# One layer of a hybrid decoder on one core: a per-layer product moved forward, and two late loads put behind the final gathers

## What is computed

```python
u = rmsnorm(h, norm_ffn)
# top group of 4, then top 2 of the 4 experts in it, weights `combine`
for e in range(N_EXPERTS):                      # 16 experts, width 256
    gu = u @ w_gate_up[e]
    hid = silu(gu[..., :D_EXPERT]) * gu[..., D_EXPERT:]
    moe = moe + combine[..., e:e+1] * (hid @ w_down[e])
h = h + moe
u = rmsnorm(h, norm_ple)                        # the per-layer input embedding
gate = sigmoid(u @ w_ple_gate)                  # 1024 x 1024
h = h + gate * (p @ w_ple_proj)                 # p has 256 columns
y = rmsnorm(h, norm_final)
```

## Time and profile before

| | us |
|---|---|
| median of 3 runs (833.25 to 833.9) | 833.69 |
| the profiled execution | 833.82 |
| its span, first to last instruction | 832.0 |
| PE busy in it | 813.1 |
| DVE, ACT and POOL busy | 384.9, 214.3, 150.8 |

### The profile page before, as it was taken

One profiled execution on the slowest core, in us unless ns is written; L12 is line 12 of the kernel. 1 busy time (PEld: TensorE's weight loads), 2 busy tenths in 40 slices (PEclk: granted clock), 3 DMA queues, 4 the chain that ended last, 5 costly groups with the idle time before them and its releaser, 6 DMA issues. The chain is left out here.

```text
span 832.0 us, 12857 instructions
## 1 busy us (share of the span) xinstructions
PE 813.1 (98%) x5198; PEld 510.2 (61%) x5198; DVE 384.9 (46%) x859; ACT 214.3 (26%) x462; POOL 150.8 (18%) x182
## 2 busy tenths in 40 slices
PE   9999999999999999999999999999899999999996
PEld 4545777887889987777777776455343333344452
DVE  3223457584666523664853559636441111005543
ACT  3211152339324311121101101123021111124554
POOL 0234321004055224200220053000100001004000
PEclk9999999999999999999999999999999999999999
DMA  9520364413020200523252024026799999986011
GB/s 355 209 101 1 109 203 152 124 48 107 4 102 3 85 19 13 202 79 94 101 202 91 11 102 179 13 90 252 298 399 399 427 419 410 417 333 218 35 39 51
DMA packets 20896, 135.23 MB, mean 163 GB/s; under 512 B 2420, under 2 KB 3060, under 8 KB 13668
## 3 DMA queue, kind: packets, MB, share of 16 engines
q1 hardware_dynamic: 13392, 103.34, 31.7%
q0 software_dynamic: 4720, 23.83, 8.0%
q10 hardware_dynamic: 2724, 7.21, 2.8%
HBM read 118.94 MB, written 19.63 MB: 167 GB/s over the span
## 5 line engine op out<-in xcount | busy, mean ns | idle before, releaser
L788 PE MATMUL pair<-mem 128*128 128x288 f32 x640 | 158.9, 408 | 0.0
L788 PEld LDWEIGHTS pair<-mem 128*128 128x128 f32 x640 | 120.3, 190 | 35.6 <-ACT mem L1423 2.1
L958 PE MATMUL single<-mem 128*128 128x288 f32 x448 | 110.0, 407 | 0.2
L958 PEld LDWEIGHTS single<-mem 128*128 128x128 f32 x448 | 84.7, 190 | 25.7 <-issue 1.6
L1333 PE MATMUL single<-mem 128*32 128x512 f32 x768 | 85.1, 594 | 0.9 <-DVE mem L2366 0.9
L1423 ACT ACTIVATE mem<-single 128x256 f32<-128x256 f32 (+5 forms) x109 | 44.6, 419 | 126.8 <-PE single L1206 48.5
L1423 ACT ACTIVATE mem<-pair 128x512 f32<-128x512 f32 (+5 forms) x77 | 33.4, 484 | 157.5 <-PE pair L788 63.1
L1402 PE MATMUL pair<-mem 128*128 128x512 f32 (+1 forms) x192 | 63.3, 524 | 0.0
L1333 PEld LDWEIGHTS single<-mem 128*32 128x32 f32 x768 | 23.6, 110 | 52.8 <-issue 51.7
L2359 DVE SCALAR_TENSOR_TENSOR mem<-single,mem 128x256 f32<-128x256 f32 x12 | 5.8, 485 | 104.0 <-PE single L1333 91.1
L1197 PE MATMUL pair<-mem 128*128 128x512 f32 x112 | 51.0, 601 | 0.0
(11 more groups left out here) (410 smaller groups left out, 1103.6 us busy)
## 6 DMA issues: line engine op xcount, KB each, us to landing
mem<-in_w_gu SPq DMA_DIRECT2D x17, 2048.0 KB, 12.7
mem<-in_w_down SPq DMA_DIRECT2D x17, 1024.0 KB, 14.0
y_slots<-mem SPq DMA_DIRECT2D x9, 512.0 KB
y_slots<-in_zeros POOLq DMA_DIRECT2D x8, 512.0 KB, 8.3
mem<-in_w_ga SPq DMA_DIRECT2D x2, 2048.0 KB, 7.7
mem<-in_w_gb SPq DMA_DIRECT2D x2, 2048.0 KB, 7.7
mem<-in_w_wo SPq DMA_DIRECT2D x2, 2048.0 KB, 7.6
mem<-in_w_pg SPq DMA_DIRECT2D x2, 2048.0 KB, 19.3
```

The source lines that it names most:

```text
L788: last = nc.tensor.matmul(pb[:, hf, 0:HALF], w(k), rhs[:, k, hf * HALF:(hf + 1) * HALF], start=(k == 0), stop=(k == kk - 1))
L958: last = nc.tensor.matmul(single[plan.buf[s]][:, 0:HALF], lhs[:, k, :], rhs[:, k, :], start=(k == 0 and j in (0, 1, 3, 4)), stop=(k == 3), ...
```

## The change

Five edits, all around the two ends of the expert phases:

- The product of tile 0, four matmuls of 512 columns (eight instructions), becomes a step `("pq", 0)` of the list, between `cnt` and the last `warm` steps, of which there are four in place of six. It writes the first bank of each `pair`, and waits for the last copy out of them and for `ld_p` at 32 (`w_proj` and `pT` have landed). ACT copies it to `pp[0]` there, in two copies of 512 columns. The p products behind the phases start with tile 1.
- The load of `pT` (576 KB) moves from behind the last expert weights (L745) to behind the load of `w_proj` (L717), with a wait for the step `("sx", 1, 2)`, whose operands lay in its new place.
- The load of `w_pg[1]` (2 MB) is no longer issued in the last phase (L748) but when the two gathers of tile 0 have landed.
- The load of `nfin` (512 KB, L750) is issued when the first tile is summed and `w_pg[1]` has landed.
- PE waits for `w_pg[0]` ahead of the first half of a gate product, and for `w_pg[1]` ahead of the second. `u3T`, `pp[0]` and `pT` get other places in SBUF.

```diff
-    ... + [("ids", z), ("cnt",)] + warm("c", [512] * 6)
+    ... + [("ids", z), ("cnt",), ("pq", 0)] + warm("c", [512] * 4)
...
-        pp = [view(RINGO + 7168 + D * ((t + 1) % NT), D) for t in range(NT)]
+        pp = [view(RINGO + 7168 + D * ((t + 1) % NT) if t else UT + 2 * D, D) for t in range(NT)]
-        pT = view(OR, 2, TOK)
+        pT = view(UT + 3 * D, 2, TOK)
-        u3T = view(UT, KD, TOK)
+        u3T = view(RINGO, KD, TOK)
...
                     sp.dma_start(w_proj.rearrange("p k c -> p (k c)"), a["w_proj"]).then_inc(sem("ld_p"), 16)
+                    mm_wait(sp, ("sx", 1, 2))
+                    sp.dma_start(pT, a["pT"]).then_inc(sem("ld_p"), 16)
...
             sp.wait_ge(sem("xT_mm"), NPH)
-            sp.dma_start(pT, a["pT"]).then_inc(sem("ld_p"), 16)
             sp.dma_start(w_pg[0], ...).then_inc(sem("w_pg"), 16)
-            sp.wait_ge(sem("gu_mm"), NPH)
-            sp.dma_start(w_pg[1], ...).then_inc(sem("w_pg"), 16)
-            sp.wait_ge(sem("dn_mm"), NPH)
-            sp.dma_start(nfin, a["norm_final"]).then_inc(sem("w_pg"), 16)
             with sp.If(n_ov > 1):
...
+            sp.wait_ge(sem("ga00"), 16)
+            sp.wait_ge(sem("ga10"), 16)
+            sp.wait_ge(sem("w_pg"), 16)
+            sp.dma_start(w_pg[1], ...).then_inc(sem("w_pg"), 16)
+            sp.wait_ge(sem("h3"), 1)
+            sp.wait_ge(sem("w_pg"), 32)
+            sp.dma_start(nfin, a["norm_final"]).then_inc(sem("w_pg"), 16)
...
+                elif k0 == "pq":                                       # on PE
+                    ev_wait(pe, ("wo", ORDER[-1], 1))
+                    pe.wait_ge(sem("ld_p"), 32)
+                    for hf in range(2):
+                        for k in range(2):
+                            last = nc.tensor.matmul(pair[hf][:, 0, :], pT[:, k, 0:P], w_proj[:, k, hf * 512:hf * 512 + 512],
+                                                    start=(k == 0), stop=(k == 1))
...
-            pe.wait_ge(sem("ld_p"), 32)
-            for t in range(NT - 1):
+            for t in range(1, NT - 1):
                 p_product(t)
...
                 pe.wait_ge(sem("u3T"), 2 * k + 2)
-                pe.wait_ge(sem("w_pg"), 48)
                 for hf in range(2):
+                    pe.wait_ge(sem("w_pg"), 16 * (hf + 1))
...
+                elif k0 == "pq":                                       # on ACT
+                    mm_wait(act, s)
+                    copy(pp[0][:, 0:512], pair[0][:, 0, :])
+                    copy(pp[0][:, 512:D], pair[1][:, 0, :]).then_inc(sem("pp"), 1)
```

More of the change, by code:

```diff
@@ L239, in schedule @@
     z = 2
-    s += warm("a", [512, 256]) + [("rank", z)] + warm("b", [256, 256]) + [("ids", z), ("cnt",)] + warm("c", [512] * 6)
+    s += warm("a", [512, 256]) + [("rank", z)] + warm("b", [256, 256]) + [("ids", z), ("cnt",), ("pq", 0)] + warm("c", [512] * 4)
     return s
@@ L261 @@
 PAIR = {"ab", "tmv", "rS", "rO", "rN", "oN", "cv", "rg", "dz", "sUs", "wo"}
-FIXED = {"ids", "wh", "wg", "sh", "tk"}
+FIXED = {"ids", "wh", "wg", "sh", "tk", "pq"}
 OWN = {"tmq", "ss", "xr"}
@@ L744, in _ @@
             sp.wait_ge(sem("xT_mm"), NPH)
-            sp.dma_start(pT, a["pT"]).then_inc(sem("ld_p"), 16)
             sp.dma_start(w_pg[0], a["w_pg0"].rearrange("k p c -> p k c")).then_inc(sem("w_pg"), 16)
-            sp.wait_ge(sem("gu_mm"), NPH)
-            sp.dma_start(w_pg[1], a["w_pg1"].rearrange("k p c -> p k c")).then_inc(sem("w_pg"), 16)
-            sp.wait_ge(sem("dn_mm"), NPH)
-            sp.dma_start(nfin, a["norm_final"]).then_inc(sem("w_pg"), 16)
             with sp.If(n_ov > 1):
@@ L755, in _ @@
                     load_ov(sp.value_load(ovi[0:1, bass.ds(i, 1)], min_val=0, max_val=NEXP - 1))
+            sp.wait_ge(sem("ga00"), 16)
+            sp.wait_ge(sem("ga10"), 16)
+            sp.wait_ge(sem("w_pg"), 16)
+            sp.dma_start(w_pg[1], a["w_pg1"].rearrange("k p c -> p k c")).then_inc(sem("w_pg"), 16)
+            sp.wait_ge(sem("h3"), 1)
+            sp.wait_ge(sem("w_pg"), 32)
+            sp.dma_start(nfin, a["norm_final"]).then_inc(sem("w_pg"), 16)
             for k, t in enumerate(LAST):
@@ L1243, in _ @@
                     last.then_inc(s_mm, 1)
+                elif k0 == "pq":
[5 more added lines that the diff above has]
+                                                    start=(k == 0), stop=(k == 1))
+                    last.then_inc(s_mm, 1)
                 elif k0 == "warm":
@@ L1359, in _ @@
                     ov_down(i)
-            pe.wait_ge(sem("ld_p"), 32)
             def p_product(t):
                 n = ntok(t)
-                if t < 2:
-                    pe.wait_ge(sem("y_ready"), 2 * NPH - 2 + 2 * t)
-                else:
+                if t == 1:
+                    pe.wait_ge(sem("y_ready"), 2 * NPH)
+                elif t > 2:
                     pe.wait_ge(sem("pp"), t - 1)
@@ L1714, in p_evac @@
             def p_evac(t):
-                act.wait_ge(sem("pp_mm"), t + 1)
+                act.wait_ge(sem("pp_mm"), t)
                 for rows, cols in sides(t):
```

## The result

The changed kernel takes 836.29 us (median of 20 executions, 832.35 to 839.41), the kernel before beside it 833.91 (20 executions, 832.95 to 835.58): the ratio is 1.0021, 95% interval [1.0012, 1.003]. It is slower by 2.4 us where 2.8 faster were forecast, and outside the range. The profiled execution of after took 837.39 us, its span is 835.6. Lines of after: the early product is L1253, the warm steps L1257, `xpose` L1282, the p products L1383, the transposes of the tail L1397, the gate products L1413, `combine` L2427, `u3_evac` L2437, the last gathers L2705.

The account below looks back on a forecast made before the run. PE alone bounds the gates; ahead of them tile 0's last store, gathers and sum end last, by 1.3 us. Tail gain 3.8 less front loss 1.0 makes 2.8 us faster: median 833.69 to 830.9, range 829.5 to 833.3.

Parts of the forecast that it names:

- Tile 0's product, the store and the gathers: Tail ahead of tile 0's transposes: one product fewer, last store landing at 743.2, gathers and sum 3.8 us earlier.
- The front: Warm stretch ahead of the experts' first transposes: eight instructions come, four go, 1.0 us lost (bounds 0.6 to 1.7).
- `pT`: Its earlier load, behind `w_proj`: the DMA engines are empty from about 555 to 566, so cost nothing.
- `nfin`: Its later load, behind `w_pg[1]`: DVE wants it only after tile 0 is gated in both halves, cost nothing.
- The landing of `w_pg[1]`: Second gate half of tile 0: load lands at 760.5, between 758.2 and 762.7, hidden by 2.3 us, cost nothing.
- the sentence on the slow engines: Within the late `w_pg[1]` case: two slower engines add 3 us, landing 763.5, stall 0.7, 831.6 us.
- The slow rival: `w_pg[1]` late at tile 0's second gate half: stall of 3.6 or 10.4 us, 834.5 or 841.3; chances 0.07 and 0.07.
- 3 us of room: Tile 1's transposes: ready at 770.2, wanted at 773.5, so gather delays of 1 to 2 us cost nothing.

Follow-up runs that it names:

- e4: Changed kernel with the load of `w_pg[1]` issued in the last phase again, as in the kernel before: 834.54 us, ratio 0.9996.
- e6: Changed kernel with two warm steps in place of four behind the early product of tile 0: 834.0 us, ratio 1.0002.
- a1_again: The changed kernel run once more without any edit, for one trace: 832.54 us.
- e3: Changed kernel with POOL holding the gathers of the third and later tiles until `w_pg[1]` has landed: 837.59 us, ratio 1.0043.
- a2_again: The changed kernel run again without any edit, for another trace: 832.3 us.
- e7: Changed kernel with third and later tiles' gathers held for `w_pg[1]`, DVE's copy of tile 1's transposes ahead of two sums, two warm steps fewer: 840.06 us.
- e8: Changed kernel with `w_pg[1]` loaded in the last phase and tile 0's product behind the phases again, six warm steps: 832.53 us, ratio 0.9975.
- e9: e4 with three unread products of 512 columns put into PE's hole ahead of the tail's first transposes: 832.6 us, ratio 0.9982.
- e10_early_filled_two_warm: e9 with two warm steps in place of four behind the early product of tile 0: 831.89 us, ratio 0.9971.

## Why the prediction was wrong, point by point

**Tile 0's product, the store and the gathers: right.** Three products, a last store of 3.41 us (3.1 forecast: from 740.07 to 743.2), POOL's first final gather at 744.27 in place of 747.71 (3.4 earlier, 2.8 expected), a wait of 1.09 us for the sum. Counted from `ids`, the transposes come at 171.99 in place of 175.25 us: 3.3 us net where 2.8 were forecast. One reading is narrower than the forecast took it: ACT's queue gets almost nothing beside SP's in the window of the earlier trace rows, but not in the windows around it. In 739.2 to 740 it moved 0.14 MB beside 0.18, and in 743 to 744 of before (packets, MB, share):

```profile
q10 hardware_dynamic: 88, 0.30, 72.8%
q1 hardware_dynamic: 44, 0.10, 26.2%
```

So the store was held at its start rather than shut out; that taking loads out of SP's queue shortens it holds all the same (7.71 us before, 5.91 in e4, where only `w_pg[1]` is back).

**The front: right.** 587.72 - 580.08 = 7.64 us from `ids` to the first transposes, 6.72 before: 0.9 lost, 1.0 forecast. e6 shows that PE was indeed the later one there, and that 0.8 of it can be had back.

**`pT`: right at nothing.** No trace shows PE waiting for it. **`nfin`: no wait either.**

**The landing of `w_pg[1]`: the step that failed.** It was put at 10.0 us after the issue, between 7.7 and 12.2. The runs show 12.6 to 16.1 beside the gathers. Two terms were too small. First, 1.76 MB of gathers ran in the first 13 us, of the tiles 1, 4 and also 2, since POOL goes on to the next tile while the load still runs. At the pace of the earlier trace rows they are 1.76 x 6.0 / 2.06 = 5.1 us, not the 4.5 at most of the forecast, and all of them count, not half: 7.7 + 5.1 = 12.8, which is a1_again's landing. Counted up to each landing, the gathers are 2.27 MB in the first trace, 1.79 in a1_again and 0.71 in e3, and the same sum gives 14.3, 12.9 and 9.8 us; measured are 16.1, 12.8 and 10.9. With 12.8 alone PE would have waited some 0.5 us, and the kernel would have been faster: the two traces with such a landing are 1.1 and 1.7 us shorter from `ids` on than that of before. Taking the middle of the bounds had no row behind it. Second, the last packets: in the first trace eleven of them, left 13.3 us after the issue, keep the whole load waiting for 2.8 us more. The forecast had the sentence on the slow engines among the rivals, on top of a middle that was too low.

**The slow rival: right place, wrong price.** It said a us for a us from a landing 12.3 us after issue. A wait of 3.92 us cost 7.2: 3.92 and 3.31 for the clock, a term that the forecast did not have. With these two terms the traces close: 251.5 - 3.3 + 3.9 + 3.3 = 255.4, measured 255.5. Its chance, 0.14, was far too small: 13 of the 20 executions took 835 us or more.

**"3 us of room" for the gathers: too wide.** Even in a1_again and a2_again PE waits 0.7 to 0.9 us for tile 2's copy, the fourth tile to be gated. The step looked at tile 1 only; e7 shows that the last gather holds back the gating of every tile through ACT's order.

**Still open.** Why the last packets come late in one execution and in time in another is not shown by any run here. That the spread of all 20 times of after comes from it rests on three traces of it, and on the narrow times of e8 and e9, where no such wait is left. It cannot be all: of the 13 executions from 835 us on, four (835.77 to 837.43) were granted 0.997, so little of their time is the clock's, and the step `ids` alone comes up to 2.5 us later in some executions than in others.

## What to carry to other kernels

When a load is taken out of a full queue, what it then runs beside must be counted to the last byte, up to the moment of its landing, and compared with when it is wanted after all the other gains of the change: here each gain in front brought the demand closer to the landing. A wait on PE can cost more than its own length where the trace shows PE without holes: here one of 3.9 us cost 7.2, while one of 2.6 us cost nothing more. Keep PE busy through it, if only with products that nobody reads, or keep a margin for the last packets. Of a change with several parts, run each alone: two small moves of loads carry all of the gain that could be told here.

## What was not expected of the hardware

- One and the same 2 MB load, issued at the same place of the same kernel, landed after 12.6, 12.8 and 16.1 us; the longest had 0.02 MB left for its last 2.2 us.
- A wait of 3.9 us on PE was followed by 3.6 us at a granted clock of 0.50 and 3.5 us at 0.64, at a cost of 3.3 us. A hole of 3.2 us left the clock at full in one trace, while eight other executions of that kernel had a lower mean clock (0.993 to 0.997) and were 1.7 to 3.9 us longer. Two waits of 1.15 and 0.85 us, one soon after the other, were followed by 3 us at 0.50 in the trace of e10_early_filled_two_warm.
- The last packets of the longest landing start 0.24 us apart, the time of one of them and of one gather packet, while most of the 16 engines stand empty.
- Rows of 16 KB in place of 2 KB made no difference to the landing of a load that shares the engines with gathers: 13.3 us.
